# Splitting five convolution weight chunks into three fp32r passes, with the first tap on ScalarE

## The reference

```python
proj = x @ w_in                                  # 1024 -> 4112
qkv, z, b_logit, a_in = jnp.split(proj, [3072, 4096, 4104], axis=-1)
qkv = jax.nn.silu(causal_depthwise_conv(qkv, w_conv))   # width 4 along the sequence
q, k, v = jnp.split(qkv, [1024, 2048], axis=-1)
q = l2_normalize(split_heads(q, nh)) * GDN_DK ** -0.5
k = l2_normalize(split_heads(k, nh))
...
o = chunk_gated_delta_rule(q, k, v, g, beta)
```

## Time and profile before

| what | value |
|---|---|
| median of 3 runs | 1957.05 us (1954.51 to 1958.12) |
| profiled execution, its time | 1954.51 us |
| profiled execution, its span | 1952.7 us |
| TensorE busy | 1874.8 us, 96% |
| VectorE busy | 912.4 us, 47% |
| ScalarE busy | 560.4 us, 29% |
| GpSimd busy | 101.0 us, 5% |
| the stage of the 24 products | 1237.9 to 1333.8 us |

### The profile page before, as it was taken

The page is one execution under the profiler, slowest core; times in us unless marked ns, Lnnn a source line. Parts: engine busy times, 40 slices in busy tenths (PEclk is TensorE's granted clock), DMA queues, the critical chain, the costliest instruction groups (busy, mean ns, idle before and its releaser), DMA issues.

```text
span 1952.7 us, 25217 instructions
## 1 busy us (share of the span) xinstructions
PE 1874.8 (96%) x10122; PEld 1115.8 (57%) x10122; DVE 912.4 (47%) x1615; ACT 560.4 (29%) x824; POOL 101.0 (5%) x120
## 2 busy tenths in 40 slices
PE   7999999999999999999999999999999999999998
PEld 5777875333333333333333333787888887878886
DVE  5764465233332332332332332567775555566544
ACT  3454441111111111111111111324444444555432
POOL 1530000000000000000000000010410000000000
PEclk9999999999999999999999999999999999999999
DMA  7342489999999999999999999334146464436452
GB/s 248 135 174 87 144 308 375 421 426 426 428 428 428 428 428 428 427 428 428 428 428 428 428 428 426 133 130 158 32 155 220 131 215 172 172 130 235 154 196 85
DMA packets 106460, 560.22 MB, mean 287 GB/s; under 512 B 5904, under 2 KB 11280, under 8 KB 81808
## 3 DMA queue, kind: packets, MB, share of 16 engines
q1 hardware_dynamic: 102528, 551.61, 70.4%
q10 hardware_dynamic: 3856, 7.53, 1.3%
HBM read 558.08 MB, written 1.05 MB: 286 GB/s over the span
## 4 chain that ended last, share of the span: by engine, by line
PE 67%; DMA 20%; DVE 6%; POOL 3%; ACT 2%; issue 2%; ACTq 0%; SPq 0%; POOLq 0%; DVEq 0%
DMA arena<-in_w_gate_up_dram 14%; PE ps L1226 12%; PE ps L885 10%; PE ps L886 9%; PE ps L887 9%; PE ps L1260 8%; DMA ring<-in_w_gate_up_dram 6%; PE ps L1342 3%; PE ps L1165 2%; PE ps L1177 2%; POOL small L822 2%; PE ps L1477 1%; PE ps L921 1%; POOL small L819 1%; PE ps L1243 1%
## 5 line engine op out<-in xcount | busy, mean ns | idle before, releaser
L1226 PE MATMUL ps<-ring,arena 128*64 128x512 f32 x1152 | 257.1, 595 | 16.7 <-DMA ring<-in_w_gate_up_dram 16.7
L2592 DVE TENSOR_SCALAR arena<-ps 128x512 f32<-128x512 f32 x32 | 22.1, 692 | 525.4 <-PE ps L1226 525.4
L2148 DVE TENSOR_TENSOR split_w<-ring,split_w 128x1024 fp32r<-128x1024 f32 (+2 forms) x176 | 203.9, 1205 | 82.1 <-ACT split_w L1942 81.6
L1226 PE MATMUL ps<-arena 128*64 128x512 f32 x896 | 203.6, 597 | 23.1 <-DMA arena<-in_w_gate_up_dram 22.8
L885 PE MATMUL ps<-split_w,act_parts 128*128 128x512 f32 (+1 forms) x544 | 209.8, 386 | 2.0 <-issue 1.0
L887 PE MATMUL ps<-split_w,act_parts 128*128 128x512 f32 (+1 forms) x544 | 205.6, 378 | 0.0
L886 PE MATMUL ps<-split_w,act_parts 128*128 128x512 f32 (+1 forms) x544 | 205.2, 377 | 0.0
L1942 ACT ACTIVATE split_w<-ring 128x1024 fp32r<-128x1024 f32 (+2 forms) x176 | 171.7, 1032 | 110.1 <-PE ps L887 110.1
L1260 PE MATMUL ps<-ring,arena 128*64 128x512 f32 x864 | 192.5, 596 | 0.0
L1226 PEld LDWEIGHTS ps<-ring,arena 128*64 128x64 f32 x1152 | 80.0, 137 | 184.2 <-issue 146.3
L1864 ACT ACTIVATE arena<-arena 128x512 f32<-128x512 f32 x32 | 20.2, 630 | 464.4 <-DVE arena L2592 464.4
(11 more groups left out here) (369 smaller groups left out, 2604.2 us busy)
## 6 DMA issues: line engine op xcount, KB each, us to landing
ring<-in_w_gate_up_dram SPq DMA_DIRECT2D x72, 2048.0 KB, 36.0
arena<-in_w_gate_up_dram SPq DMA_DIRECT2D x56, 2048.0 KB, 35.9
ring<-in_w_down_dram SPq DMA_DIRECT2D x54, 2048.0 KB, 39.3
ring<-in_f_w_dram SPq DMA_DIRECT2D x28, 2048.0 KB, 8.0
ring<-in_w_in_dram SPq DMA_DIRECT2D x14, 2048.0 KB, 7.9
arena<-in_w_down_dram SPq DMA_DIRECT2D x10, 2048.0 KB, 40.2
ring<-in_a_w_in_dram SPq DMA_DIRECT2D x8, 2048.0 KB, 7.9
ring<-in_b_w_qkv_dram SPq DMA_DIRECT2D x6, 2048.0 KB, 7.9
```

The lines of the kernel that those rows point to most:

```text
L1226: mm = pe.matmul(ps[half, bank, :], xeT[:, 2 * c + j, :], w[:, j, col:col + 512], start=False, stop=(c == 3 and j == 1), skip_group_check= ...
L2148: dve.tensor_tensor(part_place(load, 1, k, n)[:, s_, :], raw_place(load, k, n)[:, s_, :], part_place(load, 0, k, n)[:, s_, :], ALU.subtract)\
```

## The change

Chunks two to six (loads 1 to 5, products 4 to 23) are split for six of their eight k tiles, in three parts of two k tiles. ScalarE casts part q of load L to fp32r at product 4(L-1)+q+1, into `split_w[0]`; VectorE subtracts, in place over the raw weights, behind the taps of that product. TensorE makes k tiles 6 and 7 of these products as plain fp32 first, then k tiles 0 to 5 by `exact`; the first product of a chunk waits for each of the three parts. Load 0 stays as it was. The high and low parts of the activations, which z needed, are now made at product 0. The first tap goes to ScalarE (a copy with a scale from memory, signalled by `tapped`), ahead of the cast and the silu of the same product. The raw chunks have three slots, so that a load waits for the chunk three before; the third slot lies in the arena. Two pairs of semaphores are merged (`gain_in` into `const_in`, `bias_cast` into `bias_split`).

```diff
+CONV_RAWS = 3
+CONV_PARTS = 3
+FIRST_PARTS = 1
+X2_PARTS = 2
+def raw_index(load):
+    return load % CONV_RAWS if load < LOAD_Z else load % len(RAW_SLOTS)
+def raw_before(load):
+    if load < LOAD_Z + 2:
+        return load - CONV_RAWS
+    return load - len(RAW_SLOTS)
+def conv_part(n):
+    load, q = n // 4 + 1, n % 4 - 1
+    return (load, q) if q >= 0 and load < LOAD_Z else None
+def conv_parts_done(load, q):
+    return X2_PARTS + CONV_PARTS * (load - FIRST_PARTS) + q + 1
...
# SyncE
             for i, src in enumerate(post):
+                done = raw_before(i)
                 if i < len(RAW_SLOTS):
                     sync.wait_ge(used[expert_chunk_in(RAW_SLOTS[i])], blocks)
+                elif i < CONV_RAWS:
+                    sync.wait_ge(used[expert_chunk_in(RING + EXTRA - 1)], blocks)
...
# TensorE
-                    pe.wait_ge(loaded2[load % len(RAW_SLOTS)], 16 * (load // len(RAW_SLOTS) + 1))
-                    for k in range(KD):
-                        at = P * (n % 4)
-                        mm = pe.matmul(ps[:, g % GB, 0:S], raw_place(load, KD, 512)[:, k, at:at + P],
-                                       actT[:, k, :], start=(k == 0), stop=(k == KD - 1))
+                    pe.wait_ge(loaded2[raw_index(load)], 16 * raw_laps(load))
+                    at = slice(P * (n % 4), P * (n % 4) + P)
+                    split_k = 2 * CONV_PARTS if load >= FIRST_PARTS else 0
+                    for k in range(split_k, KD):
+                        mm = pe.matmul(ps[:, g % GB, 0:S], raw_place(load, KD, 512)[:, k, at],
+                                       actT[:, k, :], start=(k == split_k),
+                                       stop=(k == KD - 1 and not split_k))
+                    for k in range(split_k):
+                        if n % 4 == 0 and k % 2 == 0:
+                            pe.wait_ge(split_ready, conv_parts_done(load, k // 2))
+                        high, low = conv_high(load)[:, k, at], conv_low(load)[:, k, at]
+                        mm = exact(ps[:, g % GB, 0:S], (high, low), (z_high[:, k, :], z_low[:, k, :]),
+                                   start=False, stop=(k == split_k - 1))
...
# ScalarE
+            def conv_cast(load, q):
+                if q == 0:
+                    act.wait_ge(loaded2[raw_index(load)], 16 * raw_laps(load))
+                    if load - 2 >= FIRST_PARTS:
+                        act.wait_ge(gemm_ready, G_QKV + 4 * (load - 2) + 4)
+                act.activation(conv_high(load)[:, 2 * q:2 * q + 2, :],
+                               raw_place(load, KD, 512)[:, 2 * q:2 * q + 2, :], ACT.Copy)\
+                    .then_inc(pre_cast, 1)
...
                 if kind == "conv":
+                    act.wait_ge(gemm_ready, G_QKV + n + 1)
+                    if n >= 2:
+                        act.wait_ge(silu_done, n - 1)
+                    act.activation(conv[:, n % 2, :], ps[:, (G_QKV + n) % GB, 0:S], ACT.Copy,
+                                   scale=taps[:, 3, n:n + 1]).then_inc(tapped, 1)
+                    if n == 0:
+                        act.wait_ge(turn_done, TURN_X2 + 4)
+                        z_high_half(0)
+                        z_high_half(1)
+                    if conv_part(n):
+                        conv_cast(*conv_part(n))
                     read_out(act, G_QKV + n)
                     act.activation((qT, kT, vT)[n // 8][:, n % 8, :], conv[:, n % 2, :], ACT.Silu)\
                         .then_inc(silu_done, 1)
-                    if n in (20, 21):
-                        z_high_half(n - 20)
...
# VectorE
+            def conv_low_part(load, q):
+                s_ = slice(2 * q, 2 * q + 2)
+                dve.wait_ge(pre_cast, PRE_QUARTERS + conv_parts_done(load, q))
+                dve.tensor_tensor(conv_low(load)[:, s_, :], raw_place(load, KD, 512)[:, s_, :],
+                                  conv_high(load)[:, s_, :], ALU.subtract).then_inc(split_ready, 1)
...
-                    dve.wait_ge(gemm_ready, g + 1)
-                    if n >= 2:
-                        dve.wait_ge(silu_done, n - 1)
-                    c = step.on(dve.tensor_scalar(y, x, taps[:, 3, n:n + 1], None, ALU.mult))
+                    dve.wait_ge(tapped, n + 1)
                     for back in (1, 2, 3):
-                        after(c)
+                        if back > 1:
+                            after(c)
...
                     ins.then_inc(gemm_free[g % GB], 1)
+                    if n == 0:
+                        z_low_half(0)
+                        z_low_half(1)
+                    if conv_part(n):
+                        conv_low_part(*conv_part(n))
```

More of the change, by code:

```diff
@@ L233, with raw_laps @@
 RAW_SLOTS = (1, 0)
+CONV_RAWS = 3
[4 more added lines that the diff above has]
+    return load % CONV_RAWS if load < LOAD_Z else load % len(RAW_SLOTS)
+def raw_laps(load):
+    return load // CONV_RAWS + 1 if load < LOAD_Z else load // 2
+def raw_before(load):
[7 more added lines that the diff above has]
+    return X2_PARTS + CONV_PARTS * (load - FIRST_PARTS) + q + 1
 def freed_after(load):
@@ L257, in freed_after @@
     return G_FFN[layer] + 24 + 2 * n + 2, None
-Z_PARTS = 6
+Z_FIRST = X2_PARTS + CONV_PARTS * (LOAD_Z - FIRST_PARTS)
+Z_PARTS = Z_FIRST + 4
 LOAD_SHAPES = [(KD, 512)] * 10
@@ L567, in program @@
         exsum = rows[:, 1224:1226]
-        loaded2 = [sem(f"loaded_second{i}") for i in range(len(RAW_SLOTS))]
+        loaded2 = [sem(f"loaded_second{i}") for i in range(CONV_RAWS)]
+        tapped = sem("gdn_first_tap")
         split_ready, w2_used, hid_split, mb_inverted = map(
@@ L650, in raw_place, with conv_low, conv_high @@
         def raw_place(load, k, n):
-            return slot(RAW_SLOTS[load % len(RAW_SLOTS)], k, n)
+            i = raw_index(load)
+            if i == len(RAW_SLOTS):
+                return arena[:, 13312:13312 + k * n].rearrange("p (k n) -> p k n", n=n)
+            return slot(RAW_SLOTS[i], k, n)
+        def conv_low(load):
+            i = raw_index(load)
+            low = rest_low[:, 0:SLOT] if i == len(RAW_SLOTS) else ring_low[:, RAW_SLOTS[i], :]
+            return low.rearrange("p (k n) -> p k n", n=512)
+        def conv_high(load):
+            return split_w[0][:, load % 2, :].rearrange("p (k n) -> p k n", n=512)
         def part_place(load, part_, k, n):
@@ L1109, in _ @@
             rows_in_order(0, 0)
-            pe.wait_ge(const_in, 16)
+            pe.wait_ge(const_in, 32)
             pe.wait_ge(r_onehot, 2)
@@ L1194, in _ @@
             turn_rows(1)
-            pe.wait_ge(bias_split, 1)
+            pe.wait_ge(bias_split, 2)
             def grouped_weights(g, j, c):
@@ L1349, in _ @@
                     if load == LOAD_Z:
-                        pe.wait_ge(loaded2[load % len(RAW_SLOTS)],
-                                   16 * (load // len(RAW_SLOTS) + 1))
+                        pe.wait_ge(loaded2[raw_index(load)], 16 * raw_laps(load))
                     for k in range(KD):
@@ L1837, in _ @@
             act.wait_ge(raw_bias_in, 64)
-            act.activation(bias_parts[:, :, :], raw_bias, ACT.Copy).then_inc(bias_cast, 1)
+            act.activation(bias_parts[:, :, :], raw_bias, ACT.Copy).then_inc(bias_split, 1)
             for tile in range(NT):
@@ L1887, in z_high_half @@
                                ACT.Copy).then_inc(pre_cast, 1)
+            def conv_cast(load, q):
[6 more added lines that the diff above has]
+                    .then_inc(pre_cast, 1)
             def z_cast(q):
                 load = LOAD_Z + 1
-                act.wait_ge(loaded2[load % len(RAW_SLOTS)], 16 * (load // len(RAW_SLOTS) + 1))
+                act.wait_ge(loaded2[raw_index(load)], 16 * raw_laps(load))
                 act.activation(part_place(0, 0, KD, 512)[:, 2 * q:2 * q + 2, :],
```

36 lines of the change are left out of this document (16 added, 20 removed).

## The result

| what | before | after |
|---|---|---|
| median | 1955.02 us (1953.43 to 1958.12, 5 runs) | 1971.29 us (1968.80 to 1977.21, 5 runs) |
| ratio, 95% interval | | 1.0085 (1.0072 to 1.0098) |
| profiled execution, time and span | 1954.51, 1952.7 us | 1969.02, 1967.2 us |

The change costs 16.3 us by the medians (1971.29 less 1955.02), 14.5 us by the two profiled executions.

What follows compares the result with a forecast made beforehand. VectorE's chain, not TensorE's 96% busy share, was taken to set the pace. Longer chain and waits, 9.7 us, plus clock falls, 6.6, made +16.3 on the 1957.05 median: 1973.4 us, range 1963 to 1982.

Steps and rivals of the forecast that it cites:

- VectorE's chain: Products 4 to 20: VectorE's dependent work, not TensorE's passes, sets the pace; 74.7 us against 66.6, +8.1.
- rival C: Products stay prepared and VectorE alone binds: 67.4 us from taps 4 to 20, run 1958.9 us; chance 0.05.
- The drain once a chunk: Before products 8, 12, 16, 20 TensorE waits for the last low part, 4.3 to 5.3 us idle.
- The tap and the restart: Last product of a chunk, 4.02 us: includes TensorE's restart 0.05, remaining tiles 0.72, link 0.60 with ScalarE's tap 0.38.
- The unit products: Products with a head's normalisation step on VectorE: 5.29 us each in q, 6.02 in k.
- Casts hidden: Fifteen ScalarE casts, 1.04 us each, run while VectorE does its three taps and cost nothing.
- The clock: TensorE's clock falls after the idle at each of four chunk boundaries, 1.65 us each, 6.6 us in all.
- Rival A: The clock holds at the chunk boundaries: only +9.7 us, run 1966.8 us; chance 0.22.
- Rival B: Half speed through the unprepared 4.2 us at each boundary: 9.7 + 16.7 us, run 1983.5; chance 0.10.
- The head: Start of the stage: VectorE's start on product 4 moves from 1257.79 to 1258.8 us, +1.0.
- the shift: After product 23 TensorE is busy without a gap, so the stage's delay is handed on whole.

Runs made afterwards that it cites:

- the first experiment: The changed kernel with every split part made one product earlier; 1955.25 us against 1955.73 for the kernel before, ratio 0.9996.
- the second experiment: The changed kernel with 32 fp32r passes filling TensorE's wait at products 8, 12, 16, 20; 1966.25 us against 1955.73 for the kernel before, ratio 1.0057.

## Why the prediction was right

It said 1973.4 us; measured are 1971.29, with +16.3 us on both sides. (The 2.1 us between them are the kernel before, 1957.05 as a median of three and 1955.02 of five.) By its own steps:

- **VectorE's chain sets the pace, TensorE's shorter products are no gain.** Shown by the first experiment: all passes, no gain. With the drain gone the kernel is near rival C, which gave 0.8 us over before from taps 4 to 20 and 1.9 in all; the run has 1.8 there (68.46 against 66.64) and ends level.
- **The drain once a chunk.** Said: 4.3 to 5.3 us of idle TensorE before products 8, 12, 16 and 20. The trace has 4.4, 4.4 and about 5.0 twice, on the low part each time. VectorE's wait for the tap there was to be 1.4 us and is 2.25 at product 8, since the six passes in it are slow. The stage without falls was to take 74.7 + 10.4 us; the kernel with passes in the idle shows 75.7 + 10.4.
- **The tap and the restart were mis-sized.** Product 4L+3 takes 4.22 us without a fall, where 4.02 were said: 0.8 us in four boundaries; 0.2 more come from the unit products (next point). Of each 0.20, 0.09 are the tap: taken as 0.38 us, it takes 0.47 (next row, a median over all 24). The other 0.1 are the six passes behind the wait, 0.82 us (1255.79 to 1256.61 at product 4) in place of 0.72, because the first is followed after 0.23 us and not after 0.12. The copy of the earlier trace rows has a constant scale; this one reads it from memory. The Trainium skill ("ScalarE: Activation LUTs", What ACT_TABLE_LOAD costs) gives 93 ns for a pointer operand, and the trace agrees: 473 less 384 is 89. Groups by line of the kernel after, duration in ns least, median, most:

```profile
L1968 ACT ACTIVATE arena<-ps,cols x24: 454/473/476, 1241.8 to 1350.7; 128x256 f32<-128x256 f32 x24
```

- **The unit products.** Said 5.29 and 6.02 us, measured 5.39 and 5.98: 4 x 0.10 more, 4 x 0.04 less. Casts hidden (L1951, 1.05 us), low parts 1.22 us: as said.
- **The clock.** Said: a fall at each of four boundaries, 6.6 us, 1.65 each. Measured: four falls (0.64, 0.57, 0.53 and 0.50 in windows there), 7.8 us. Behind the idles of 4.4 us they cost 1.34 and 1.60 us, less than the one of the earlier trace rows; behind those of 5.00 us 2.87 and 1.98. Rival A, no fall, would have been the second experiment, and that is 10.5 us over its before, where A said 9.7. Rival B, half speed throughout, would have cost 16.7 us and is refuted by the 7.8, and at product 8 by the pitch of 0.12 us from 1277.5 on.
- **The head.** Said +1.0 us at product 4, seen -0.5 (1257.32 against 1257.79). The row that the term was read from was itself late: two windows of before, 1236 to 1244, have a clock of 0.86 and 0.72, those of after 1.00. TensorE starts product 0 at 1237.88 and 1237.75, and the first tap of that product starts 5.43 us later before (on VectorE), 4.04 after (on ScalarE). Kernels with the same instructions up to there show the same: 4.04 or 4.05 us where the clock is 1.00 (five of the experiments), 5.11 in the first experiment (0.80 and 0.77). So nearly all of the 1.5 us lies ahead of product 0's first tap and goes with the clock. From that tap to VectorE's start on product 4 the changed kernel takes 15.53 us against 14.48, the 1.0 more that was said.

Against the profiled executions (+14.5) the sum is 1.8 us too high: 1.0 (chain) and 1.2 (falls) too little in the stage, 1.5 too much at the head, and 2.4 of the shift not arriving at the end. Against the medians it is exact, so the number is better than its terms: the mechanism was right, and that the sum meets the medians to 0.1 us is luck.

**What stays open.** Outside the 20 products the profiled executions differ by falls that no edit explains: the clock in 1236 to 1244 is 0.58 and 0.56 with the tap back on VectorE and 1.00 in the changed kernel, with the same instructions up to there but the tap. The passes in the idle were profiled at 1961.14 us while the other three runs took 1966.1 to 1967.6. So a profile and a median can stand 5 us apart, and the versions that win 3 to 7 us show 0.8 to 7.3 of it between taps 4 and 23.

The traces place much of the rest. Counted from TensorE's start on product 0 to its first pair product, the stage takes 95.75 us before, and 91.54, 88.98 and 88.61 without parts, with two parts and with the low part in GpSimd's wait: 4.2, 6.8 and 7.1 us less, where the medians say 4.2, 6.5 and 6.8. What varies lies around it. Product 0 starts anywhere from 1237.2 to 1240.75 us. From the first pair product to the end eight of the twelve traces take 616.7 to 617.4 us and four 618.8 to 619.1, and these four, that of before among them, have a fall (0.60 to 0.66 in a window of 4 us) between 1404 and 1420. Why the clock falls there in some executions and not in others was not settled.

## What to carry to other kernels

When one engine prepares operands for another in line with its own chain, see that the last piece is ready one full step before use: here the index of the part was worth 16 us, and TensorE, which may run up to three products ahead, lost that lead once a chunk and its clock with it. Ask of a split which engine has the room for its preparation before counting the passes it saves; here the passes paid (2.4 us) only after VectorE's unit products had been cut from 5.4 to 4.2 us, and more than half of what the fastest versions gain came from ScalarE's order without any pass. And work put into another engine's waiting time has to be asked what it shares with the engine that is waited for.

## What the runs showed of the hardware that was not expected

VectorE's subtraction with both inputs in SBUF stretches a GpSimd operation on 4 elements a partition from 0.19 to 1.10 us when the two meet (8 of 8), and not when it is elsewhere (8 of 8 at 0.19 or 0.20). The second GpSimd operation, 1.01 us, began when the subtraction had ended and was not stretched. The Trainium skill ("SBUF — State Buffer", Who interferes with whom) says that a VectorE instruction with two SBUF inputs contends with a GpSimd instruction that reads SBUF; the trace agrees, and the expectation of that run had overlooked it.

The falls differ in length with the same kind of wait: behind 4.41 us of idle the low clock lasts some 3.6 us (1273.82 to 1277.4), behind 4.93 us the clock is 0.51 and 0.63 in the next two windows of 4 us. And a fall costs only where TensorE has nothing done ahead: 7.8 us for the four of the changed kernel, nothing for the two of the first experiment, through which VectorE kept its spacing of 5.98 and 2.85 us.
